# Causal attention of a decoder step on one Trainium2 core: value products over both column halves of the array, denominators added up on VectorE and GpSimd

## The chip, the core and the metric

The kernel runs on one core of one Trainium2 chip: TensorE (matrix products, with its weight loads shown as an engine of their own, PEld), VectorE (DVE), ScalarE (ACT), GpSimd (POOL) and the DMA queues that SyncE (SP) and the others issue. The metric is the device time of one execution in microseconds.

## The reference

One inference step of a one-layer hybrid decoder: 4096 prompt tokens (and 8 sample tokens) pass an RMSNorm and one input projection; the results feed causal attention with a forget gate (6 heads of 64), a state-space group and a cross-attention over 256 memory tokens; an output projection joins them. The change touches only the causal attention over the prompt:

```python
def fox_attend(q, c_q, q_pos, k, v, c_k):
    s = jnp.einsum('bqhd,bkhd->bhqk', q, k).astype(jnp.float32) * (HEAD_DIM ** -0.5)
    s = s + jnp.swapaxes(c_q, 1, 2)[..., :, None] - jnp.swapaxes(c_k, 1, 2)[..., None, :]
    causal = jnp.arange(k.shape[1])[None, :] <= q_pos[:, None]
    s = jnp.where(causal, s, -jnp.inf)
    p = jax.nn.softmax(s, axis=-1)
    return jnp.einsum('bhqk,bkhd->bqhd', p.astype(v.dtype), v)
```

Here c is the running sum of the log forget gates. All is in float32.

## The kernel before

The program is a chain of stages with a barrier between them: `project_prompt`, `forget_gates`, `fox_prompt` (the attention), `memory_prompt`, `ssm`, `sample_attend`, `mix_out`. Only `fox_prompt` changes. It runs from about 1151 us to 2677 us of the span.

For each of 6 heads the queries are cut into 8 blocks of 512 columns (`b`), the keys into 32 tiles of 128 rows (`j`). Block `b` needs tiles 0 to 4b+3, so a head has 144 tiles, 6 heads 864. On the last four tiles of each block only the columns from `q0` = 0, 128, 256, 384 on are computed: of the 864 tiles 720 are 512 wide and 48 each are 384, 256 and 128 wide. Each tile passes three engines:

- TensorE, scores: two products into one of two banks, L1020 (split keys `kst` by the high part `qhi` of the queries) and L1021 (`kone` by the rest `qlo`, whose row 64 carries the negated maximum of each query), and on diagonal tiles a mask (L1023).
- ScalarE, L951: exponential of the bank into one of three buffers `p`.
- TensorE, value product, L1004 in `weighted`: `vone` holds 64 value columns and 64 columns of ones, so that one float32 product of the tile gives outputs on partitions 0 to 63 and the denominators on 64 to 127, summed in a bank of 512 columns. Each float32 product appears in the trace as two MATMUL records.

The maximum of each query must be known before its block starts. `first_pass` (L991) computes the scores once more with the queries on the partitions, in 144 chunks a head, into three banks in turn (`NPRE` = 3); VectorE takes each chunk's maximum (`maxima`, L872) and frees the bank; the four maxima of a block (L876) are turned into a row by TensorE (L979), copied (L879 `mrow`) and brought into `qlo` by a DMA of SyncE (L776). TensorE issues up to three chunks behind each score tile, for the block after the next; in the last block of a head and before its start the chunks of the next head's first blocks.

At a block's end `finish` on VectorE takes the reciprocal of the denominators (L885, 64x512), multiplies (L887), applies the gate (L891), and SyncE stores. `split_q` (L855, L857, L858), `split_k` (L847, L849) and `k_one` (L864) prepare operands, also on VectorE. TensorE's order is score tile n, chunks, value product of tile n-1. Five heads run in a loop, the sixth is written out.

GpSimd meanwhile computes the constant tables of the state-space stage (`ssm_c.tables`, most of it through the helper line L285): many small instructions and some of up to 1024 columns.

## Time and profile before

| What | us |
|---|---|
| median of 3 runs (4040.92 to 4050.84) | 4041.15 |
| the profiled execution, its own time | 4048.91 |
| its span (first to last instruction) | 4047.3 |
| TensorE busy, whole span | 3509.0 (87%) |
| VectorE busy, whole span | 1693.8 (42%) |
| ScalarE busy, whole span | 1008.7 (25%) |
| GpSimd busy, whole span | 652.7 (16%) |

Busy times of one engine overlap for a matmul and the next, so TensorE's share says that it has work in flight, not how full the array is. The granted TensorE clock is 0.901 of full speed over the span. The attention is a bit over a third of the span, and its engines are read there, in stretches, and not from the page's averages.

### The profile page before, as it was taken

The page shows a single profiled execution, that of the slowest core. Times are in us where ns is not written, and L with a number is a line of the kernel's source. Part 1 is how long each engine was busy: PE and PEld are TensorE (multiplying, and loading weights), DVE is VectorE, ACT ScalarE, POOL GpSimd, SP SyncE. Part 2 cuts the span into 40 slices and gives each one's busy share as a digit, 9 for nine tenths or more (in the row PEclk, how much of TensorE's full clock was granted, in tenths as well). Part 3 has the DMA queues.
Part 4 walks back from the last instruction along what each step waited for, and adds up shares of the span by engine and source line. Part 5 has one row for each costly group of instructions (what it writes and reads, how often), then busy time and mean ns, then how long its engine had stood idle before and what let it go on. Part 6 is the DMA issues. An engine that isn't in the chain of part 4 may idle for free. (4 is left out here: it accounts for less than half of the span.)

```text
span 4047.3 us, 44763 instructions
## 1 busy us (share of the span) xinstructions
PE 3509.0 (87%) x14216; PEld 2459.2 (61%) x14216; DVE 1693.8 (42%) x2594; ACT 1008.7 (25%) x1791; POOL 652.7 (16%) x1265
## 2 busy tenths in 40 slices
PE   5999999999949989999899999967767766598999
PEld 4987879879835545555555555534335542376766
DVE  4132131141137567374664747427534542323232
ACT  1112121111113433434344343423201110212120
POOL 0000000000047776500000000000046620000000
PEclk9998999989969999999999999987786777698989
DMA  3241232322141122210101001032156541442322
GB/s 100 94 141 71 86 125 90 124 84 94 68 71 49 50 70 79 61 26 20 39 20 34 22 18 30 3 122 62 42 164 177 157 139 51 121 125 86 124 86 73
DMA packets 236613, 323.67 MB, mean 80 GB/s; under 512 B 100484, under 2 KB 168748, under 8 KB 235380
## 3 DMA queue, kind: packets, MB, share of 16 engines
q1 hardware_dynamic: 175028, 203.79, 17.8%
q10 hardware_dynamic: 49488, 68.48, 4.6%
q0 software_dynamic: 11904, 48.87, 3.6%
q8 instruction: 116, 1.90, 0.2%
q14 instruction: 77, 0.63, 0.0%
HBM read 221.37 MB, written 99.61 MB: 79 GB/s over the span
## 5 line engine op out<-in xcount | busy, mean ns | idle before, releaser
L1004 PE MATMUL bank<-p,vone 128*128 128x512 f32 (+1 forms) x1728 | 862.2, 581 | 10.3 <-ACT p L951 9.7
L951 ACT ACTIVATE p<-bank,ncol 128x512 f32<-128x512 f32 (+1 forms) x864 | 562.1, 651 | 817.0 <-PE bank L1021 647.1
L1020 PE MATMUL bank<-qhi,kst 128*128 128x512 f32 (+1 forms) x864 | 644.0, 745 | 14.1 <-issue 12.6
L872 DVE TENSOR_REDUCE pm<-bank 128x1 f32<-128x512 f32 (+2 forms) x864 | 516.9, 640 | 264.1 <-PE bank L991 195.2
L535 PE MATMUL bank<-xhi,whi 128*128 128x512 f32 x1024 | 408.0, 398 | 7.0 <-DVE xlo L502 7.0
L535 PE MATMUL bank<-xlo,whi 128*128 128x512 f32 x1024 | 406.9, 397 | 0.0
L535 PE MATMUL bank<-xhi,wlo 128*128 128x512 f32 x1024 | 406.9, 397 | 0.0
L1004 PEld LDWEIGHTS bank<-p,vone 128*128 128x128 f32 x1728 | 321.4, 198 | 72.7 <-issue 13.3
L991 PE MATMUL bank<-kone,qone 66*128 66x512 f32 (+2 forms) x864 | 294.6, 413 | 61.6 <-DVE qlo L858 33.9
L476 DVE CAST whi<-wraw 128x3072 fp32r<-128x3072 f32 (+2 forms) x32 | 52.1, 1629 | 703.5 <-PE bank L535 703.5
L1021 PE MATMUL bank<-qlo,kone 66*128 66x512 f32 (+1 forms) x864 | 335.9, 389 | 0.0
L1020 PEld LDWEIGHTS bank<-qhi,kst 128*128 128x128 f32 x864 | 169.2, 196 | 194.4 <-issue 163.2
L1021 PEld LDWEIGHTS bank<-qlo,kone 66*128 66x128 f32 x864 | 169.0, 196 | 177.7 <-issue 170.9
L885 DVE RECIPROCAL rec<-bank 64x512 f32<-64x512 f32 x48 | 161.2, 3359 | 229.4 <-PE bank L1004 228.3
L991 PEld LDWEIGHTS bank<-kone,qone 66*128 66x128 f32 x864 | 166.5, 200 | 111.9 <-issue 53.8
L535 PEld LDWEIGHTS bank<-xhi,whi 128*128 128x128 f32 x1024 | 194.5, 190 | 54.1 <-issue 8.6
L535 PEld LDWEIGHTS bank<-xlo,whi 128*128 128x128 f32 x1024 | 195.1, 191 | 46.1
L535 PEld LDWEIGHTS bank<-xhi,wlo 128*128 128x128 f32 x1024 | 194.5, 190 | 45.7
L2198 PE MATMUL bank<-wo_hi,mx_hi 128*128 128x512 f32 x512 | 205.6, 402 | 0.8 <-DVE wo_raw L2104 0.8
L2198 PE MATMUL bank<-wo_lo,mx_hi 128*128 128x512 f32 x512 | 203.2, 397 | 0.0
L2198 PE MATMUL bank<-wo_hi,mx_lo 128*128 128x512 f32 x512 | 203.1, 397 | 0.0
L569 ACT ACTIVATE fstage<-bank 128x512 f32<-128x512 f32 x104 | 62.2, 598 | 524.3 <-PE bank L535 524.3
(387 smaller groups left out, 4725.5 us busy)
## 6 DMA issues: line engine op xcount, KB each, us to landing
wraw<-in_w_in SPq DMA_DIRECT2D x20, 1536.0 KB, 6.7
ssm_consts<-gp POOLq DMA_DIRECT2D x6, 3080.0 KB, 10.2
x_tok<-in_x_prompt SPq DMA_DIRECT2D x8, 2048.0 KB, 11.2
gate_t<-fstage ACTq DMA_DIRECT2D x32, 512.0 KB, 2.6
mx_x<-in_x_prompt SPq DMA_DIRECT2D x32, 512.0 KB, 3.5
out_y_prompt<-mx_xo ACTq DMA_DIRECT2D x32, 512.0 KB, 2.9
q<-q_t SPq DMA_DIRECT2D x96, 128.0 KB, 3.0
ssm_turns<-ssm_consts SPq DMA_DIRECT2D x24, 512.0 KB, 3.7
```

The source lines that it names most:

```text
L476: dve.tensor_copy(whi[:, si % 2, :, 0:w], wraw[:, :, 0:w]).then_inc(whi_done, 1)
L535: last = pe.matmul(dst, lhsT, rhs, start=(k == 0 and ws is whi and xs is xhi), stop=(k == KD - 1 and ws is wlo))
L569: act.activation(fstage[:, slot, 512 * h:512 * (h + 1)], bank[:], func, scale=1.0 if scale is None else scale).then_inc(evac_done, 1)
L872: dve.tensor_reduce(pm[:, r, ch:ch + 1], c.bank[XB + n % NPRE][:, 0:w], AX.X, ALU.max).then_inc(pre_max, 1)
L885: dve.reciprocal(rec[:], ob[HD:P, :]).then_inc(o_rec, 1)
L951: act.activation(p[:, n % 3, q0:512], c.bank[n % SB][:, q0:512], ACT.Exp, bias=ncol[:, j:j + 1]).then_inc(ex, 1)
L991: mm = pe.matmul(bank[:, 0:w], qone[:, b % QS, q], kone[:, 512 * ch:512 * ch + w], start=True, stop=True)
L1004: pe.matmul(c.bank[OB + b % 2][:, q0:512], vone[:, j, :], p[:, n % 3, q0:512], start=(j == 0), stop=(j == 4 * b + 3), skip_group_check=Tru ...
L1020: pe.matmul(bank[:, q0:512], kst[:, j * P:(j + 1) * P], qhi[:, b % QS, q0:512], start=True, stop=False)
L1021: mm = pe.matmul(bank[:, q0:512], kone[:, j * P:(j + 1) * P], qlo[:, b % QS, q0:512], start=False, stop=True)
L2198: mm = pe.matmul(c.bank[4 + 2 * (t % 2) + h][:], ms_[:, j, k, t * P:(t + 1) * P], ws_[:, k, 512 * h:512 * (h + 1)], start=(k == 0 and ws_ ...
```

## The change

`fox_prompt` is rewritten in steps of four tiles. In words:

- A value product is two products of 64 stationary columns (`v_tok`, without the ones) and at most 256 moving columns: query columns 0 to 255 of the block go to output partitions 0 to 63, columns 256 to 511 to partitions 64 to 127 of the same bank (`weighted`). A tile whose `q0` is 256 or more has only the second. The order on TensorE is: four score tiles with their chunks, then the four value products of the step before.
- The denominators are no longer part of the product. VectorE adds each tile of `p` into `acc_dve` (`add_up`; the first tile of a block is copied); in heads 3 to 5, from block 1 on, the tiles with j % 4 == 1 (105 in all) are added by GpSimd into `acc_pool` and `merge` adds the two. Two products with ones (`denominators`) then sum over the partitions. GpSimd starts on its share behind the tables.
- `finish` works on 128x256 in place of 64x512.
- `p` has 12 buffers in place of 3; the queries have 5 in place of 4.
- A table (`FoxPlan`) places the 144 chunks of a head: they begin 20 tiles ahead, at a rate of 1.14 to a tile, so that tiles 106 to 123 of each head have none. The row of maxima of blocks 5, 6 and 7 is turned in the step before the block's first, in the other blocks earlier.
- All six heads are written out; `split_k` is cut into eight pieces.

The diff, cut to its core:

```diff
+class FoxPlan:
+    STEP = 4
+    def __init__(self, nh, nb, lead, num, den):
+        self.nb = nb
+        self.main = [(b, j, max(0, (j - 4 * b) * P)) for b in range(nb) for j in range(4 * b + 4)]
+        self.pre = [(b, r, ch, 512 if ch < b else (r + 1) * P) for b in range(nb) for r in range(4) for ch in range(b + 1)]
+        self.per = len(self.main)
+        assert len(self.pre) == self.per
+        self.total = nh * self.per
+        self.blocks = nh * nb
+        self.start = [sum(4 * x + 4 for x in range(b)) for b in range(nb + 1)]
+        self.chunks_at, self.rows_at, self.split_at = {}, {}, {}
+        for g in range(self.blocks):
+            h, b = divmod(g, nb)
+            when = [max(-1, self.per * h + (m * den) // num - lead) for m in range(self.start[b], self.start[b + 1])]
+            for m, t in zip(range(self.start[b], self.start[b + 1]), when):
+                self.chunks_at.setdefault(t, []).append(self.per * h + m)
+            self.rows_at.setdefault(when[-1] // self.STEP + 1 if when[-1] >= 0 else -1, []).append(g)
+            self.split_at.setdefault(when[0] // self.STEP - 1 if when[0] >= self.STEP else -1, []).append(g)
+            assert when[-1] // self.STEP + 1 < self.first(g) // self.STEP or g == 0
...
+    QS, PS, GS = 5, 12, 4
+    plan = FoxPlan(NF, NB, 20, 114, 100)
+    NMN, PER, NBLK = plan.total, plan.per, plan.blocks
+    POOL_FROM = 3
+    STEP, NST = plan.STEP, plan.total // plan.STEP
+    def on_pool(n):
+        h, b, j, q0 = plan.tile(n)
+        return h >= POOL_FROM and b > 0 and j % STEP == 1
+    pool_done, dve_done = [0], [0]
+    for n in range(NMN):
+        pool_done.append(pool_done[-1] + on_pool(n))
+        dve_done.append(dve_done[-1] + (not on_pool(n)))
...
-        vone = sb("vone", [P, NT, P])
-        gate = sb("gate_a", [HD, T])
-        ncol = sb("ncol", [P, NT])
-        p = sb("p", [P, 3, 512])
+        vt = sb("v_tok", [P, NT, HD])
+        gate = sb("gate_a", [P, GS, 256])
+        p = sb("p", [P, PS, 512])
+        accd, accp = sb("acc_dve", [P, 2, 512]), sb("acc_pool", [P, 2, 512])
...
-        rec = sb("rec", [HD, 512])
-        on = sb("on", [HD, 512])
-        og = sb("og", [HD, 2, 512])
+        rec = sb("rec", [P, 256])
+        on = sb("on", [P, 256])
+        og = sb("og", [P, 2, 256])
...
+            for n in range(NMN):
+                if not on_pool(n):
+                    continue
+                h, b, j, q0 = plan.tile(n)
+                g = NB * h + b
+                pool.wait_ge(ex, n + 1)
+                k = pool_done[n]
+                if j == 1:
+                    if g >= 2:
+                        pool.wait_ge(merged, g - 1)
+                    pool.tensor_copy(accp[:, g % 2, :], p[:, n % PS, :]).then_inc(accp_done, 1)
+                else:
+                    pool.wait_ge(accp_done, k)
+                    pool.tensor_tensor(accp[:, g % 2, q0:512], accp[:, g % 2, q0:512], p[:, n % PS, q0:512], ALU.add
+                                       ).then_inc(accp_done, 1)
...
+            def add_up(n):
+                h, b, j, q0 = plan.tile(n)
+                g = NB * h + b
+                if not on_pool(n):
+                    dve.wait_ge(ex, n + 1)
+                    k = dve_done[n]
+                    if j == 0:
+                        if g >= 2:
+                            dve.wait_ge(den, g - 1)
+                        dve.tensor_copy(accd[:, g % 2, :], p[:, n % PS, :]).then_inc(accd_done, 1)
+                    else:
+                        dve.wait_ge(accd_done, k)
+                        dve.tensor_tensor(accd[:, g % 2, q0:512], accd[:, g % 2, q0:512], p[:, n % PS, q0:512], ALU.add
+                                          ).then_inc(accd_done, 1)
+            def merge(g):
+                n1 = plan.end(g)
+                dve.wait_ge(accd_done, dve_done[n1])
+                if on_pool(n1 - 3):
+                    dve.wait_ge(accp_done, pool_done[n1])
+                    dve.tensor_tensor(accd[:, g % 2, :], accd[:, g % 2, :], accp[:, g % 2, :], ALU.add).then_inc(merged, 1)
+                else:
+                    dve.sem_inc(merged, 1)
+            def finish(g):
+                ob = c.bank[OB + g % 2]
+                dve.wait_ge(den, g + 1)
+                dve.reciprocal(rec[:], ob[:, 256:512]).then_inc(o_rec, 1)
+                dve.wait_ge(o_rec, g + 1)
+                dve.tensor_tensor(on[:], ob[:, 0:256], rec[:], ALU.mult).then_inc(o_norm, 1)
+                dve.wait_ge(o_norm, g + 1)
+                dve.wait_ge(g_in[g % GS], 32 * (g // GS + 1))
+                if g >= 2:
+                    dve.wait_ge(o_stored[g % 2], 32 * (g // 2))
+                dve.tensor_tensor(og[:, g % 2, :], on[:], gate[:, g % GS, :], ALU.mult).then_inc(o_gated, 1)
...
+            for m in range(NST):
+                h, b, j, q0 = plan.tile(STEP * m)
+                for n in range(STEP * m, STEP * (m + 1)):
+                    for x in plan.chunks_at.get(n, []):
+                        maximum(x)
+                for x in (plan.rows_at.get(m, []) if m else []):
+                    row(x)
+                for x in plan.split_at.get(m, []):
+                    split_q(x)
+                if m:
+                    for n in range(STEP * (m - 1), STEP * m):
+                        add_up(n)
+                    if plan.ended(m - 1):
+                        merge(plan.block(m - 1))
+                if m >= 2 and plan.ended(m - 2):
+                    finish(plan.block(m - 2))
+                if h + 1 < NF and b == NB - 1:
+                    split_k(h + 1, j // KG)
+                    if j >= KG:
+                        k_one(h + 1, j // KG - 1)
+                if h and b == 0:
+                    k_one(h, NG - 1)
...
+            for n in range(NMN):
+                h, b, j, q0 = plan.tile(n)
+                act.wait_ge(sc, n + 1)
+                if n >= PS:
+                    act.wait_ge(pv, n - PS + 1)
+                    act.wait_ge(accd_done, dve_done[n - PS + 1])
+                    if pool_done[n - PS + 1]:
+                        act.wait_ge(accp_done, pool_done[n - PS + 1])
+                act.activation(p[:, n % PS, q0:512], c.bank[n % SB][:, q0:512], ACT.Exp, bias=c.negc[:, h, j:j + 1]).then_inc(ex, 1)
...
+            def weighted(n):
+                h, b, j, q0 = plan.tile(n)
+                g = NB * h + b
+                pe.wait_ge(ex, n + 1)
+                if j == 0 and g >= 2:
+                    pe.wait_ge(o_norm, g - 1)
+                for hf in range(2):
+                    lo, hi = max(q0, 256 * hf), 256 * (hf + 1)
+                    if lo < hi:
+                        mm = pe.matmul(c.bank[OB + g % 2][HD * hf:HD * (hf + 1), lo - 256 * hf:256], vt[:, j, :], p[:, n % PS, lo:hi],
+                                       start=(j == 0), stop=(j == 4 * b + 1 + 2 * hf), skip_group_check=True)
+                mm.then_inc(pv, 1)
+            def denominators(g):
+                pe.wait_ge(merged, g + 1)
+                for hf in range(2):
+                    mm = pe.matmul(c.bank[OB + g % 2][HD * hf:HD * (hf + 1), 256:512], c.ones[:, 0:HD],
+                                   accd[:, g % 2, 256 * hf:256 * (hf + 1)], start=True, stop=True, skip_group_check=True)
+                mm.then_inc(den, 1)
...
+            def values(m):
+                if m and plan.ended(m - 1):
+                    denominators(plan.block(m - 1))
+                for n in range(STEP * m, STEP * (m + 1)):
+                    weighted(n)
...
-            ROWS_AT = (13, 18, 26)
...
+                for x in (plan.rows_at.get(m, []) if m else []):
+                    maxima_to_rows(x)
+                for n in range(STEP * m, STEP * (m + 1)):
+                    h, b, j, q0 = plan.tile(n)
...
+                    for x in plan.chunks_at.get(n, []):
+                        first_pass(x)
+                if b == NB - 1 and h + 1 < NF and j > KG:
+                    turn_k(h + 1, j // KG - 1)
+                if h and b == 0:
+                    turn_k(h, NG - 1)
+                if m:
+                    values(m - 1)
+            values(NST - 1)
+            denominators(NBLK - 1)```

Where the instructions stand. TensorE before, in the last block of the loop's body: a score tile of two products (L1020, L1021) and one value product (L1004) in turn.

```order
L1004 MATMUL bank<-p,vone 128x512
L1020 MATMUL bank<-qhi,kst 128x512
L1021 MATMUL bank<-qlo,kone 128x512
L1001 REGISTER_ALU
L1004 MATMUL bank<-p,vone 128x512
L1020 MATMUL bank<-qhi,kst 128x512
L1021 MATMUL bank<-qlo,kone 128x512
```

And now one step on TensorE, in block 5 of the second head (L1141 and L1142 are the score products, L1087 the chunks, L1103 the value products):

```order
L1141 MATMUL bank<-qhi,kst 128x512
L1142 MATMUL bank<-qlo,kone 128x512
L1087 MATMUL bank<-kone,qone 128x512 x2
L1141 MATMUL bank<-qhi,kst 128x512
L1142 MATMUL bank<-qlo,kone 128x512
L1087 MATMUL bank<-kone,qone 128x512
L1141 MATMUL bank<-qhi,kst 128x512
L1142 MATMUL bank<-qlo,kone 128x512
L1087 MATMUL bank<-kone,qone 128x512
L1141 MATMUL bank<-qhi,kst 128x512
L1142 MATMUL bank<-qlo,kone 128x512
L1087 MATMUL bank<-kone,qone 128x512
L1103 MATMUL bank<-p,v_tok 64x256 x8
```

The value products have gathered at the step's end, eight of 64x256 where four of 128x512 stood between the score tiles.

VectorE, around the end of a block: before, maxima, and the three instructions of `finish` between them.

```order
L871 REGISTER_ALU
L872 TENSOR_REDUCE pm<-bank 128x1
L883 REGISTER_ALU
L885 RECIPROCAL rec<-bank 64x512
L887 TENSOR_TENSOR on<-bank,rec 64x512
L888 REGISTER_ALU
L890 REGISTER_ALU
L891 TENSOR_TENSOR og<-on,gate_a 64x512
L871 REGISTER_ALU
L872 TENSOR_REDUCE pm<-bank 128x1
```

And now (L938 is a maximum, L949 the row's copy, L960 and L963 the adding up, L978 to L985 `finish`):

```order
L938 TENSOR_REDUCE pm<-bank 128x1 x4
L949 CAST mrow<-bank 4x128
L960 COPY acc_dve<-p 128x512
L963 TENSOR_TENSOR acc_dve<-acc_dve,p 128x512 x3
L978 RECIPROCAL rec<-bank 128x256
L980 TENSOR_TENSOR on<-bank,rec 128x256
L985 TENSOR_TENSOR og<-on,gate_a 128x256
L938 TENSOR_REDUCE pm<-bank 128x1 x5
L963 TENSOR_TENSOR acc_dve<-acc_dve,p 128x512 x4
```

Between two groups of maxima VectorE now has four additions to make, and the next chunks of TensorE wait for the maxima behind them.

## Rows read from the trace of the kernel before

**Rows 1.** Table by stretch: before, during and after the attention's tile loop.

```profile
core 0: us, PE busy (x) PEld busy (x) DVE busy (x) ACT busy (x) POOL busy (x), PEclk, DMA share, GB/s
1160.00:1210.00 50.00, 24.70 (x78) 15.35 (x78) 29.37 (x61) 4.78 (x8) 29.40 (x73) 0.50 0.56 89
1210.00:2672.00 1462.00, 1373.85 (x4873) 824.65 (x4873) 858.81 (x1297) 590.55 (x909) 364.71 (x810) 0.96 0.13 36
```

**Rows 2.** Waits in 1210 to 2670 us: total, times, longest (us).

```profile
ACT p L951 <- PE bank L1021: 647.1, 630, 7.8
DVE pm L872 <- PE bank L991: 193.4, 259, 8.5
...
PE bank L991 <- DVE pm L872: 10.5, 18, 1.3
```

**Rows 3.** Timeline of TensorE late in the last head: start us, us, instruction.

```profile
2655.74 1.02 PE L1004 MATMUL bank<-p,vone 128*128 128x512 f32 x2
2656.20 0.79 PE L1020 MATMUL bank<-qhi,kst 128*128 128x512 f32 x1
...
2657.07 1.02 PE L1004 MATMUL bank<-p,vone 128*128 128x512 f32 x2
```

**Rows 4.** The same with two chunks (L991) to a tile.

```profile
2052.24 1.02 PE L1004 MATMUL bank<-p,vone 128*128 128x512 f32 x2
...
2053.58 0.63 PE L991 MATMUL bank<-kone,qone 66*128 66x512 f32 x2
2054.04 0.59 PE L1004 MATMUL bank<-p,vone 128*128 128x512 f32 x1
```

**Rows 5.** Timeline of TensorE in the memory stage: four products on alternate row halves.

```profile
2767.66 1.13 PE L1276 MATMUL bank<-mem_kt,mem_q 64*128 64x256 f32 x8
```

**Rows 6.** Timeline of VectorE, no GpSimd work beside it.

```profile
1999.70 1.29 DVE L872 TENSOR_REDUCE pm<-bank 128x1 f32<-128x512 f32 x2 [0.72 <-PE bank L991]
...
2004.34 0.40 DVE L855 CAST qhi<-q 128x512 fp32r<-128x512 f32 x1
2004.78 0.42 DVE L857 CAST qone<-qhi 64x512 fp32r<-64x512 f32 x1
2005.12 0.68 DVE L858 TENSOR_TENSOR qlo<-q,qhi 64x512 fp32r<-64x512 f32 x1
```

**Rows 7.** Groups by shape on VectorE: out<-in xcount | busy us, mean ns | idle before.

```profile
L872 DVE TENSOR_REDUCE pm<-bank 128x1 f32<-128x512 f32 x720 | 466.8, 685 | 212.9 <-PE bank L991 195.2 <-PE bank L994 17.3
L885 DVE RECIPROCAL rec<-bank 64x512 f32<-64x512 f32 x48 | 161.2, 3359 | 229.4 <-PE bank L1004 228.3
L872 DVE TENSOR_REDUCE pm<-bank 128x1 f32<-128x384 f32 x48 | 26.5, 552 | 15.0 <-PE bank L994 14.8
L872 DVE TENSOR_REDUCE pm<-bank 128x1 f32<-128x256 f32 x48 | 20.3, 422 | 21.7 <-PE bank L994 21.6
L864 DVE CAST kone<-kst 64x512 fp32r<-64x512 f32 x48 | 19.8, 412 | 0.0
L872 DVE TENSOR_REDUCE pm<-bank 128x1 f32<-128x128 f32 x48 | 13.5, 282 | 14.5 <-PE bank L994 14.5
```

**Rows 8.** The subtraction L858 (two SBUF inputs): ns min/median/max, to 1640 us and after 1900 us.

```profile
L858 DVE TENSOR_TENSOR qlo<-q,qhi x18: 675/774/2818, 1166.6 to 1625.8; 64x512 fp32r<-64x512 f32 x18
...
L858 DVE TENSOR_TENSOR qlo<-q,qhi x22: 675/676/679, 1908.5 to 2550.1; 64x512 fp32r<-64x512 f32 x22
```

**Rows 9.** Timeline of GpSimd and VectorE over one such meeting.

```profile
1512.38 2.40 POOL L285 TENSOR_TENSOR gp<-gp,st_big 128x1024 f32<-128x1024 f32 x1
1512.51 2.82 DVE L858 TENSOR_TENSOR qlo<-q,qhi 64x512 fp32r<-64x512 f32 x1
```

**Rows 10.** GpSimd while it makes the tables (us, busy (x), clock), and its 512-wide addition.

```profile
1160.00:1700.00 540.00, 394.11 (x882) 0.91 0.22 63
...
L285 POOL TENSOR_TENSOR gp<-gp,st_big 128x512 f32<-128x512 f32 x12 | 15.7, 1310 | 0.9
```

**Rows 11.** Table by stretch, a piece of the memory stage; columns as in rows 1.

```profile
2800.00:2900.00 100.00, 77.56 (x326) 41.79 (x322) 71.66 (x162) 33.23 (x131) 0.00 (x0) 0.79 0.24 56
```

More of the change, by code:

```diff
@@ L809, in _ @@
+            load_k(0)
+            load_q(0)
+            load_q(1)
             sp.wait_ge(ones_set, 5)
@@ L932, in _ @@
+            for g in range(NG):
+                split_k(0, g)
+            split_q(0)
+            split_q(1)
+            dve.wait_ge(ones_set, 5)
+            for g in range(NG):
                 k_one(0, g)
             ssm_c.copy_c(dve, c)
-            heads(dve, body)
+            for g in plan.split_at[-1][2:]:
+                split_q(g)
+            for m in plan.chunks_at[-1]:
+                maximum(m)
+            for g in plan.rows_at[-1]:
+                row(g)
+            for m in range(NST):
+                h, b, j, q0 = plan.tile(STEP * m)
+                for n in range(STEP * m, STEP * (m + 1)):
[18 more added lines that the diff above has]
+                    k_one(h, NG - 1)
@@ L936, in _ @@
+            for n in range(STEP * (NST - 1), NMN):
+                add_up(n)
+            merge(NBLK - 1)
+            if plan.ended(NST - 2):
+                finish(NBLK - 2)
+            finish(NBLK - 1)
         @block.scalar
@@ L998, in weighted @@
[L998 to L1017 removed]
+                turns[0] += 1
@@ L1045, in body @@
-                    if n:
-                        weighted(h, n - 1)
-                    if j == 4 * b + 3 and rows_due:
-                        maxima_to_rows(h, b + 2, NG * (h + 1))
-                    if b == LASTB and not last and j and j % KG == 0:
-                        rows = sum(x < j for x in ROWS_AT)
-                        if rows > sum(x < j - KG for x in ROWS_AT):
-                            pe.wait_ge(mrow_done, NB * (h + 1) + rows)
-                        turn_k(h + 1, j // KG - 1)
```

397 lines of the change are left out of this document (166 added, 231 removed).

## Prediction, as put on record before the changed kernel ran

> **What bounds the kernel now.** Start with the table by stretch [rows 1]: the tile loop of the attention takes 1462 us, 36% of the span, and TensorE has work in flight for 1374 of them, VectorE for 859, ScalarE for 591. The clock there is 0.96. The other stages are untouched, so the forecast is this stretch's new length; the setup ahead of it is only reordered and I leave it at nothing. The waits [rows 2] say the same from the other side: ScalarE waits 647 us for scores and VectorE 193 for chunks, while TensorE waits 10.5 for the maxima. TensorE ends last everywhere.
>
> Next, what TensorE's time consists of. Where no chunks run, a tile comes every 1.33 us (2655.74 to 2657.07) [rows 3]; with two chunks every 1.80 (2052.24 to 2054.04) [rows 4]. So a 512-column chunk costs 0.235, the two score products, of the same width, 0.47, and the float32 value product the remaining **0.86 us**. In 512-column equivalents there are 720 + 48 x (0.75 + 0.5 + 0.25) = 792 value products: 681 us, half of the stretch. That is what the change goes for.
>
> **TensorE after.** Whether two half-width products run at once is seen in the memory stage: four float32 products of 256 columns on alternate row halves take 1.13 us together [rows 5]. One behind another they would be 4 x 0.43 = 1.72. Each is two records of 0.215; if the second record of one runs beside the first of the next, five slots are 1.08, and that is about what stands there. I take the same for column halves: nearest row, though no row shows column halves. Terms:
> - the value products fall to half: -341;
> - tiles with q0 of 256 and 384 fill one half only, so save nothing: 48 x (0.43 + 0.215) / 2 = +15;
> - each of the 216 steps of four ends with one record alone (0.215) and empties the array twice, going to half width and back. A product's record is 0.40 long where its successor starts after 0.235 [rows 3, 4], so emptying shows some 0.165; with two of them 0.545 a step, +118 (bounds: 0 and 0.545);
> - denominators: 48 pairs of 0.645, +31.
> 1374 - 341 + 15 + 118 + 31 = **1197 us**, 5.5 a step.
>
> **VectorE after.** It had 603 us to spare and now gets the denominators. All prices are for a full queue, where instructions follow at once:
> - maxima, 864: starts lie 0.61 apart (two end after 1.29, one lasts 0.685) [rows 6, 7]; the narrow ones at their mean less the same 0.08: 720 x 0.61 + 48 x (0.47 + 0.34 + 0.20) = 488;
> - additions: the nearest row has two SBUF inputs and 512 columns, 0.676 [rows 8], and an instruction that waits for the one before starts 0.035 after its end [rows 6]: 0.71. Narrower ones less 0.13 per 128 columns, the slope of the maxima [rows 7]. GpSimd takes 105 tiles (84 full, 21 of 384); 48 are copies. 588 x 0.71 + 27 x 0.58 + 48 x 0.45 + 48 x 0.31 = 470;
> - copies as L855 at 0.44: 21; 21 merges at 0.71: 15;
> - finish: a reciprocal of 512 columns is 3.36 [rows 7], so of 256 columns 1.72 with its wait, and two products of 0.45: 48 x 2.62 = 126 (228 before). If the reciprocal did not scale with columns it would be 79 more;
> - unchanged: L855 to L858 at 0.44 + 0.34 + 0.64 [rows 6], 68; L864 20 [rows 7]. Rows of maxima 21 and key pieces of 256 columns 48 x 0.75 = 36, both priced by the narrow rows of [rows 7].
> Sum: **1265 us**, 5.9 a step. So VectorE becomes the engine that ends last, 68 us above TensorE. In the queue, the next chunks' maxima stand behind the additions, and TensorE behind the maxima, with three banks of lead. While VectorE adds (2.8 us), TensorE makes its value products (2.3), then three chunks with their scores (2.1): it arrives first, and VectorE finds three chunks waiting. So the engines do overlap in steady state, and the sum is a good floor there. Twelve buffers of `p` cover ScalarE's lead, and ScalarE (0.69 a tile, 2.8 a step) is never last.
>
> **What the floor lacks.** First, GpSimd. While it works on its tables [rows 10], L858 takes 0.774 in the median in place of 0.676, up to 2.818 [rows 8]. The rows of one meeting show why: beside a table instruction of 2.40 it waits 2.14 of its 2.82 [rows 9], so about the other's length less 0.26. The 882 table instructions are 394 us busy [rows 10]; if each were met by an addition, it would cost 394 - 882 x 0.25 = 174 us (upper bound; lower bound 0). They come every 0.61 us. In a step there are four additions, each letting one of them through, and some 3 us of maxima, which read PSUM and let five pass. Four ninths of 174 is 78: **+80**, spread over the first 98 steps or so, before GpSimd's own share starts with the fourth head (step 108). The 105 additions on GpSimd (about 1.31 each [rows 10]) come while VectorE is at maxima, and I cost them at nothing; without that cover they would cost up to 105 x 1.06 = 111. The Trainium skill has a rule against this change here (SBUF — State Buffer, § SBUF: two separate sides): the port pair that VectorE and GpSimd share is an exclusive lock for an instruction with two SBUF inputs, and the loser blocks for the whole of it. The long meeting agrees; the narrow ones cost 0.10, less than the 0.34 of such an instruction. By the rule in full, with every addition met, the sum would have 174 where I put 80.
>
> Second, places where neither engine's sum holds: the row of maxima of blocks 5 and 6 is made one step before the block, and its DMA (issue 0.7, some 2 to land, by the other small ones: an estimate) keeps TensorE until about the end of the additions, so that VectorE waits 1.3: 12 times, 16. The last 38 tiles have no chunks, TensorE's 4.1 a step against 2.7: 14. The first short blocks of each head with a row, a finish and a split nearly every step, 5 a head: 25 with the remainder; and in heads 3 to 5 VectorE (5.5 a step) and TensorE (5.5) are level, so each one's delays pass to the other: 10. Together **+65**.
>
> Sum: 1265 + 80 + 65 = 1410 against 1462, -52. The profiled execution's own time of 4048.9 becomes 3997; it is 7.8 above the median shown, from which I count: 4041.2 - 52 = **3989 us**.
>
> **Rivals.**
> 1. Tighter than I think (0.18). The emptying costs little, additions mostly meet narrow table instructions (40), and the unequal places cost 30: 1265 + 70 = 1335, 3914. For it: the long table instructions, which carry the excess, are few. Against it: GpSimd always has the next one ready.
> 2. GpSimd decides (0.20): slower. Every table instruction of length meets an addition, 174 in place of 80, for 1504 and **4083**. The gain is gone from the point where the meetings cost over 132, three quarters of the bound. For it: L855, L857 and L858 in a row each waited in turn, as in [rows 9], and additions come in rows of four. Against it: 5 of 9 table instructions have the maxima to run in. The TensorE clock could do the same: where TensorE had pauses, in the memory stage, its clock was 0.79 [rows 11] against 0.96 in the loop [rows 1], and it will have pauses of about 0.4 a step. At 0.8 its 1197 become some 1440 and 4070 is reached.
> 3. The column halves do not run together, so the change doesn't do what it says (0.10). Then TensorE has 1374 + 216 x 0.33 + 48 x 0.86 = 1487, with 65 for waits 1552: +90, **4131**. Against it: the row halves [rows 5].
>
> **How the numbers follow.** The forecast has 0.52, rivals 0.18, 0.20 and 0.10. 0.3% of the time, about what a measurement can tell, is 12 us. The forecast's own range is 3925 to 4045 (table meetings 0 to 130, places 40 to 90), of which 0.07 lies within the 12 us: faster 0.45 + 0.18, about 0.63; same 0.08; slower 0.29. The range for 8 in 10 takes in most of rivals 1 and 2 and leaves the third out: **3900 to 4100**.
>
> **What would show it.** Right: VectorE over 90% busy in the loop and TensorE's longest waits on the maxima (L938); L1103's eight records of a tile pair in about 0.43 us a tile; additions (L963) of 0.68 after step 110 and of 0.8 and more before, some over 2; tables ending later than before, at some 700 us after the loop's start; the loop at about 1410. Wrong: value products that need 0.86 a tile (rival 3); VectorE with gaps of a microsecond before maxima in most steps, or a clock under 0.9 in the loop; a reciprocal over 2 us.

## The result: 0.45% slower, and the profile after

| What | before | after |
|---|---|---|
| median of 8 runs each, us | 4046.27 (4040.92 to 4055.53) | 4065.9 (4048.62 to 4075.19) |
| ratio | | 1.0045, 95% interval 1.003 to 1.006 |
| the profiled execution, its own time | 4048.9 | 4066.9 |
| its span | 4047.3 | 4065.2 |
| tile loop, first score product to last gate product | 1463.4 | 1481.7 |
| granted TensorE clock over the span | 0.901 | 0.873 |

The forecast was 3989 (3900 to 4100), faster. The range holds the result; the sign is wrong. The loop alone explains the difference: it is 18 us longer, the median 20. Everything that follows is about these 1482 us, against the 1410 that I had worked out for them.

The table by stretch of the changed kernel, cut at the starts of heads 0, 1, 2 and 3 (heads are counted from 0); columns as in [rows 1]:

```profile
core 0: us, PE busy (x) PEld busy (x) DVE busy (x) ACT busy (x) POOL busy (x), PEclk, DMA share, GB/s
1205.00:1486.00 281.00, 226.34 (x1092) 137.06 (x1092) 243.33 (x362) 97.03 (x151) 221.66 (x408) 0.82 0.18 57
1486.00:1769.00 283.00, 223.54 (x1114) 134.89 (x1112) 251.55 (x377) 97.71 (x152) 208.67 (x370) 0.84 0.18 57
1769.00:2014.00 245.00, 217.52 (x1117) 132.80 (x1113) 214.26 (x378) 97.55 (x152) 0.00 (x0) 0.87 0.11 27
2014.00:2687.00 673.00, 603.90 (x3288) 370.72 (x3288) 586.15 (x996) 287.81 (x449) 117.72 (x105) 0.93 0.10 24
```

Heads 0 and 1 take 281 and 283 us, head 2 takes 245, heads 3 to 5 together 673. The kernel before needed 251, 252, 244 and 717 for the same. So nothing is won in head 2, 44 us are won in the last three heads, and 61 are lost in the first two, where GpSimd is busy with its tables. VectorE is busy for 1295 us of the 1482 (87%), where it was 859 [rows 1].

The waits in the loop say who holds whom (total us, times, longest), and stand against [rows 2]:

```profile
ACT p L1048 <- PE bank L1142: 585.0, 276, 8.0
...
PE bank L1087 <- DVE pm L938: 147.9, 76, 8.4
...
DVE pm L938 <- PE bank L1087: 62.4, 93, 2.3
...
DVE khl L912 <- DMA ktok<-out_k_prompt: 14.2, 5, 3.7
```

TensorE now waits 148 us for the maxima, where it waited 10.5; VectorE still waits 62 for chunks. VectorE's groups by shape in the loop (xcount | busy us, mean ns | idle before), which answer to [rows 7]:

```profile
L963 DVE TENSOR_TENSOR acc_dve<-acc_dve,p 128x512 f32<-128x512 f32 x588 | 470.1, 799 | 53.7 <-ACT p L1048 8.7 <-DVE acc_dve L963 1.4
L938 DVE TENSOR_REDUCE pm<-bank 128x1 f32<-128x512 f32 x706 | 454.9, 683 | 76.9 <-PE bank L1087 62.4 <-PE bank L1090 6.5 <-DVE nm L943 0.5
L978 DVE RECIPROCAL rec<-bank 128x256 f32<-128x256 f32 x48 | 84.0, 1751 | 6.0 <-PE bank L1110 5.3
```

The additions (L963) are as dear as the maxima. Of the idle time before them, 53.7 us, only 10 has a releaser. The timeline of VectorE in head 4, with no table instruction anywhere, shows what the rest is (start us, us, instruction):

```profile
2302.70 2.47 DVE L938 TENSOR_REDUCE pm<-bank 128x1 f32<-128x512 f32 x4
...
2305.29 2.26 DVE L963 TENSOR_TENSOR acc_dve<-acc_dve,p 128x512 f32<-128x512 f32 x3
2307.47 2.67 DVE L938 TENSOR_REDUCE pm<-bank 128x1 f32<-128x512 f32 x5
```

Four maxima, which overlap, end after 2.47: (2.47 - 0.69) / 3 = 0.59 apart. Three additions need 2.26: (2.26 - 0.69) / 2 = 0.79 apart, longer than each of them lasts. Over the loop the median distance of two 512-wide additions in a row is 0.796 us (390 pairs; with the narrower ones of the diagonal tiles there are 507): each waits for the sum that the one before it writes, and starts 0.10 us after its end. Counted over the loop, with those behind a block's first copy and before a merge, 563 such gaps hold 57 us.

Beside the tables it is a different matter. VectorE and GpSimd in one step of head 0:

```profile
1250.66 9.09 DVE L963 TENSOR_TENSOR acc_dve<-acc_dve,p 128x512 f32<-128x512 f32 x4
1259.68 2.34 DVE L938 TENSOR_REDUCE pm<-bank 128x1 f32<-128x512 f32 x4
```

```profile
1249.88 1.90 POOL L285 TENSOR_TENSOR gp<-gp,uc 128x1024 f32<-128x1024 f32 x1
1251.86 2.23 POOL L285 TENSOR_TENSOR st_big<-gp,us 128x1024 f32<-128x1024 f32 x1
1254.17 2.73 POOL L285 TENSOR_TENSOR gp<-gp,st_big 128x1024 f32<-128x1024 f32 x1
1256.98 2.23 POOL L285 TENSOR_TENSOR gp<-gp,uc 128x1024 f32<-128x1024 f32 x1
```

Four additions take 9.09 us in place of 3.1, since each lets one table instruction of 1024 columns pass. The four maxima right behind, which read PSUM, take their usual 2.34 beside two more such instructions.

GpSimd waits as well. Its most frequent table instruction in the kernel before, and in the changed one:

```profile
L285 POOL TENSOR_TENSOR gp<-gp,st_big 128x64 f32<-128x64 f32 x156 | 53.0, 340 | 12.2
```

```profile
L285 POOL TENSOR_TENSOR gp<-gp,st_big 128x64 f32<-128x64 f32 x156 | 64.9, 416 | 12.2
```

All its table instructions together (885 and 884 from 1100 us on) are busy for 478 us where they were 402. That the additions do this shows in run 6 below, which has none: there the 884 table instructions take 395 us.

TensorE does what was forecast. The four value products of a step in head 4:

```profile
2303.86 1.95 PE L1103 MATMUL bank<-p,v_tok 128*64 128x256 f32 x16
2305.74 0.50 PE L1141 MATMUL bank<-qhi,kst 128*128 128x512 f32 x1
```

16 records in 1.88 until the next product starts: 0.47 us a tile in place of 0.86.

### The profile page after: what moved, and what is told of

Its sections match the earlier page's. It is cut to its first block and busy times, and to the rows that moved or that the text cites. A ratio compares the mean times of both kernels' runs of the same rounds, so it can differ in the third digit from the quotient of the medians.

```text
span 4065.2 us, 46870 instructions
## 1 busy us (share of the span) xinstructions
PE 3408.6 (84%) x15944; PEld 2409.0 (59%) x15944; DVE 2131.4 (52%) x3410; ACT 1001.1 (25%) x1787; POOL 844.5 (21%) x1369
## 3 DMA queue, kind: packets, MB, share of 16 engines
q1 hardware_dynamic: 182708, 203.80, 17.7%
## 5 line engine op out<-in xcount | busy, mean ns | idle before, releaser
L1048 ACT ACTIVATE p<-bank,negc 128x512 f32<-128x512 f32 (+1 forms) x864 | 557.0, 652 | 874.7 <-PE bank L1142 585.0
L938 DVE TENSOR_REDUCE pm<-bank 128x1 f32<-128x512 f32 (+2 forms) x864 | 513.3, 638 | 92.0 <-PE bank L1087 62.4
L963 DVE TENSOR_TENSOR acc_dve<-acc_dve,p 128x512 f32<-128x512 f32 (+3 forms) x711 | 520.0, 731 | 66.9 <-ACT p L1048 9.1
L1087 PE MATMUL bank<-kone,qone 66*128 66x512 f32 (+2 forms) x864 | 365.4, 440 | 174.1 <-DVE pm L938 152.5
L1103 PE MATMUL bank<-p,v_tok 128*64 128x256 f32 (+1 forms) x3264 | 489.9, 434 | 0.0
L1141 PE MATMUL bank<-qhi,kst 128*128 128x512 f32 (+1 forms) x864 | 394.4, 456 | 27.7 <-DMA qlo<-mrow 18.9
L1103 PEld LDWEIGHTS bank<-p,v_tok 128*64 128x64 f32 x3264 | 265.9, 157 | 189.4 <-issue 89.3
L1142 PE MATMUL bank<-qlo,kone 66*128 66x512 f32 (+1 forms) x864 | 341.6, 395 | 0.0
L1087 PEld LDWEIGHTS bank<-kone,qone 66*128 66x128 f32 x864 | 178.7, 209 | 246.1 <-DVE pm L938 183.1
L1141 PEld LDWEIGHTS bank<-qhi,kst 128*128 128x128 f32 x864 | 173.8, 201 | 163.9 <-ACT p L1048 64.8
L900 POOL TENSOR_TENSOR acc_pool<-acc_pool,p 128x512 f32<-128x512 f32 (+1 forms) x84 | 104.8, 1248 | 407.3 <-ACT p L1048 407.3
```

The source lines that it names most:

```text
L900: pool.tensor_tensor(accp[:, g % 2, q0:512], accp[:, g % 2, q0:512], p[:, n % PS, q0:512], ALU.add).then_inc(accp_done, 1)
L938: dve.tensor_reduce(pm[:, r, ch:ch + 1], c.bank[XB + m % NPRE][:, 0:w], AX.X, ALU.max).then_inc(pre_max, 1)
L963: dve.tensor_tensor(accd[:, g % 2, q0:512], accd[:, g % 2, q0:512], p[:, n % PS, q0:512], ALU.add).then_inc(accd_done, 1)
L1048: act.activation(p[:, n % PS, q0:512], c.bank[n % SB][:, q0:512], ACT.Exp, bias=c.negc[:, h, j:j + 1]).then_inc(ex, 1)
L1087: mm = pe.matmul(bank[:, 0:w], qone[:, g % QS, r * P:(r + 1) * P], kone[:, 512 * ch:512 * ch + w], start=True, stop=True)
L1103: mm = pe.matmul(c.bank[OB + g % 2][HD * hf:HD * (hf + 1), lo - 256 * hf:256], vt[:, j, :], p[:, n % PS, lo:hi], start=(j == 0), stop=(j = ...
```

## The experiments

The theory after this look: **VectorE sets the loop, and three things lengthen its queue**: additions that wait for one another, additions that wait for table instructions, and times in which it has no finished chunk. The rivals: the new order costs TensorE more than I counted, or its clock does; or it is the placing of the chunks.

In the table, "against the change" is the ratio less 1.0045, times 4046 us. Two intervals go into each, so that it is good to about 12 us. "Loop" is from the profiled execution, counted as above. The runs came in three groups of four; the kernel before ran beside each group (medians of 4043.7, 4047.6 and 4047.9 us), and the ratios are to that.

| Kernel | median us | ratio to before (95%) | against the change | loop |
|---|---|---|---|---|
| 1 five of six table rounds left out | 3996.9 | 0.9875 (0.9849 to 0.9901) | -69 | 1425 |
| 2 two accumulators in turn | 3968.5 | 0.9808 (0.9782 to 0.9833) | -96 | 1385 |
| 3 additions between the maxima | 3999.1 | 0.9878 (0.9851 to 0.9906) | -68 | 1421 |
| 4 both halves on the same columns | 4172.0 | 1.0315 (1.0288 to 1.0342) | +109 | 1588 |
| 5 kernel before, tables as in 1 | 4041.2 | 0.9981 (0.9969 to 0.9993) | | 1447 |
| 6 no additions | 3824.0 | 0.9445 (0.9425 to 0.9464) | -243 | 1230 |
| 7 as 2, GpSimd from head 2 on | 3967.8 | 0.9788 (0.9764 to 0.9812) | -104 | 1384 |
| 8 as 7, GpSimd two tiles of four | 3970.8 | 0.9798 (0.9776 to 0.9820) | -100 | 1394 |
| 9 chunks at 1.30 a tile | 4052.1 | 1.0010 (0.9993 to 1.0027) | -14 | 1468 |
| 10 as 1 and 2 together | 3902.6 | 0.9645 (0.9611 to 0.9678) | -162 | 1319 |
| 11 as 2 and 3 together | 3973.4 | 0.9809 (0.9783 to 0.9835) | -96 | 1392 |
| 12 as 2, GpSimd adds nothing | 3987.0 | 0.9848 (0.9821 to 0.9874) | -80 | 1408 |

### 1 and 5: the table instructions, and their control

```diff
-        for g0 in range(0, G, m_):
+        for g0 in (0,):
```

The one result is stored for all groups.

> The changed kernel with one of the six rounds of GpSimd's table work left: the other five rounds are left out, so the state-space outputs are not the reference's. Theory GpSimd (the meetings of additions with table instructions made heads 0 and 1 of the changed kernel 281 and 283 us long against 245 for head 2, which has no GpSimd work): heads 0 and 1 fall to about 245 to 250, total -65 to -75, near 3995. Rival (the row of maxima, the clock or the burst order cost the time in heads 0 and 1): less than -20.

> The kernel before, with five of the six rounds of GpSimd's table loop left out (their results are replaced by the first round's, so the state-space part of the output is not the reference's). It is the control of the run with few tables. Theory A (the 69 us that the changed kernel won without the tables come from additions of VectorE that meet table instructions): the kernel before has hardly any two-input instructions on VectorE in the loop and TensorE ends last, so it gains under 5 us: 4039 to 4046 beside a before of about 4044, with a loop of 1460 to 1465. Theory B (the tables cost something that has nothing to do with the additions, as HBM traffic or a lower TensorE clock): it gains a good part of the 69 too, 3980 to 4020.

-69 us for the changed kernel, as expected, and -8 for the kernel before (4046 x 0.0019), a little over the 5 that theory A allowed and nothing like the 24 to 64 of theory B. So about 60 us of the 69 belong to the changed kernel alone. The loops of the profiled executions give less: 57 us and, for the kernel before, 16 (1447, where 1460 to 1465 were expected), which leaves 41. Each loop is that of a single execution, and 13 executions of the kernel before spread over 21 us. That it is VectorE's instructions meeting table instructions, additions above all, is seen in their lengths: what all its instructions of heads 0 and 1 last over the median of their shape in head 2 falls from 76 us to 10. Head 0 falls from 281 to 257 us, head 1, which has no table instruction left, from 283 to 242. Its VectorE shows additions at their own length (head 1 of run 1, one line of the groups), where the same line of heads 0 and 1 of the changed kernel has a mean of 950:

```profile
L964 DVE TENSOR_TENSOR acc_dve<-acc_dve,p 128x512 f32<-128x512 f32 x112 | 77.1, 689 | 8.8
```

```profile
L963 DVE TENSOR_TENSOR acc_dve<-acc_dve,p 128x512 f32<-128x512 f32 x219 | 207.9, 950 | 17.7 <-DVE acc_dve L963 0.5
```

### 2: two accumulators in turn

```diff
-        accd, accp = sb("acc_dve", [P, 2, 512]), ...
+        accd, accp = sb("acc_dve", [P, 4, 512]), ...
...
-                        dve.wait_ge(accd_done, k)
-                        dve.tensor_tensor(accd[:, g % 2, q0:512], ...
+                        dve.wait_ge(accd_done, k - 1 if b else k)
+                        dve.tensor_tensor(accd[:, d, q0:512], ...
```

`d` alternates between two buffers of the block, so that the first two tiles of a block are copied and not the first alone (90 copies and 546 additions of 512 columns in place of 48 and 588); `denominators` issues its products for both and sums them in the bank.

> VectorE adds alternate tiles into two accumulators, and TensorE sums both, so that no addition reads what the one before wrote. Theory dependency (an addition behind an addition starts 0.794 us after it, where I had priced 0.71, since it waits for the semaphore of its predecessor): starts fall to about 0.61 to 0.65, as the maxima's, and the total by 60 to 90 us less some 30 of added products on TensorE that is partly idle: 3980 to 4020. Rival (VectorE and TensorE take turns in bursts of four, and VectorE's saving only becomes more waiting for chunks): -25 or less.

Of the single changes that keep the additions it gains most, -96 us, and more than the expected 3980 to 4020 allowed. The timeline of VectorE in this run:

```profile
2290.12 1.29 DVE L938 TENSOR_REDUCE pm<-bank 128x1 f32<-128x512 f32 x2
2291.32 1.89 DVE L965 TENSOR_TENSOR acc_dve<-acc_dve,p 128x512 f32<-128x512 f32 x3
2293.12 3.07 DVE L938 TENSOR_REDUCE pm<-bank 128x1 f32<-128x512 f32 x5
```

Three additions end after 1.89 in place of 2.26: 0.602 apart in the median, as close as maxima. 0.796 - 0.602 = 0.194 for each of the 563 pairs would be 109; 96 came out, and of these some 11 belong to the 42 tiles that are copied now (in this run the next instruction starts 0.34 us after a copy and 0.60 after an addition). An estimate for the dependence alone is thus 85 us. The gaps between additions fall from 57 to 3 us.

### 3 and 11: each addition behind one tile's maxima

```diff
                     for x in plan.chunks_at.get(n, []):
                         maximum(x)
+                    if m:
+                        add_up(n - STEP)
...
-                    for n in range(STEP * (m - 1), STEP * m):
-                        add_up(n)
```

> VectorE's order alone is changed: behind each tile's maxima one addition of the step before, in place of all maxima of a step and then four additions. It takes away the dependent pairs and the bursts at once. Theory bursts: -60 to -100 us and TensorE's waits for maxima (148 us in the loop) fall under 60. If only the dependency counts: about the same as the two accumulators, -50. Rival GpSimd: more additions meet table instructions since they are spread over the whole step, heads 0 and 1 stay at 280.

> Two accumulators in turn and, besides, each addition behind one tile's maxima in place of four in a row. Theory A (with independent additions nothing is left for the interleaving to take away, and the finer order only lets VectorE run out of finished chunks more often, 151 us of large idle times against 109 in the run that interleaved alone): no gain or a loss, 3965 to 3985 beside the 3968.5 of the run with two accumulators. Theory B (additions between maxima meet fewer table instructions in a row and free the banks earlier, so TensorE stops less in the first two heads): 3935 to 3955.

Run 3 takes the waits between additions away by other means (gaps of 57 us fall to 9), and gains 68, not 96. TensorE's waits for the maxima fall from 148 us to 91, not under 60, and heads 0 and 1 take 250 and 262 us, so they did not stay at 280. VectorE's waits of over 0.15 us grow from 109 to 151 us, which I put down to its asking for chunks earlier in each step; no run separates this. Run 11 adds nothing to two accumulators, as theory A said: both changes cure the same cost.

### 4: do the column halves run together?

```diff
-                        mm = pe.matmul(c.bank[OB + g % 2][HD * hf:HD * (hf + 1), ...
+                        mm = pe.matmul(c.bank[OB + g % 2][HD * (hf if j == 0 else 0):HD * ((hf if j == 0 else 0) + 1), ...
```

From the second tile of each block on, both halves go to partitions 0 to 63, so the value sums are not the reference's; the count and width of all products is the same.

> From the second tile of each block on, both halves of a value product go to partitions 0 to 63, so both use the same column half of the array; the outputs are wrong. If column halves do run together in the changed kernel: a step's 16 records take about 3.5 us in place of 1.95, TensorE ends last, and the total rises by 150 to 250 us. If they did not run together, nothing changes.

+109 us, less than the expected 150 to 250. The four value products of a step (TensorE, head 4) now need 3.18 in place of 1.95 (expected: 3.5):

```profile
2320.27 3.18 PE L1103 MATMUL bank<-p,v_tok 128*64 128x256 f32 x16
```

0.80 us a tile against 0.49: the halves do run together in the changed kernel. In head 3 of this run TensorE ends last again, at a granted clock of 0.98:

```profile
2070.00:2320.00 250.00, 242.38 (x1120) 152.79 (x1122) 202.05 (x351) 97.90 (x153) 38.39 (x35) 0.98 0.12 26
```

### 6: TensorE's own floor

```diff
+    def adds(n):
+        return plan.tile(n)[2] == 0
```

`add_up` is called for these tiles alone, the first of each block; the other 816 additions are left out, on both engines, and with them the 21 merges. The first tile's copy is written as an addition of a constant.

> The changed kernel without its additions: of each block only the first tile goes into the accumulator, the other 816 tiles are left out of the denominators, on VectorE and on GpSimd, so the outputs are not the reference's. What is left is TensorE's own floor. Theory A (the new TensorE order is cheap, VectorE's additions hold it back): VectorE's sum falls by some 440 us below TensorE's, and the loop is about what I had put for TensorE with small waits, 1197 + 40 to 60 = 1240 to 1260 in place of 1482, the whole 3820 to 3850. Theory B (TensorE in the new order has stalls of its own, by emptying twice a step or by the row DMA): the loop stays above 1330, the whole above 3915.

3824 us, with a loop of 1230. The loop by stretch (head 0, head 1, heads 2 to 5):

```profile
1205.00:1428.00 223.00, 205.24 (x1092) 128.20 (x1092) 147.46 (x234) 96.93 (x151) 170.73 (x380) 0.89 0.20 60
1428.00:1634.00 206.00, 192.90 (x1116) 121.30 (x1114) 139.58 (x242) 97.53 (x152) 150.11 (x371) 0.98 0.24 75
1634.00:2435.00 801.00, 758.35 (x4399) 478.20 (x4398) 510.81 (x903) 385.19 (x601) 29.90 (x35) 0.97 0.13 32
```

TensorE needs some 200 us a head where it hardly waits for VectorE (22 us for maxima over the loop). My sum for it was 1197, the loop is 33 more, a little less than the 40 to 60 that I expected for its waits. The additions, their merges included, are the whole loss: 252 us of the changed kernel's loop go with them.

### 9: are the chunks placed too unevenly?

```diff
-    plan = FoxPlan(NF, NB, 20, 114, 100)
+    plan = FoxPlan(NF, NB, 20, 130, 100)
```

> The changed kernel with its chunks spread at a rate of 1.30 to a tile in place of 1.14 (the same work, only placed more unevenly: some 33 of 144 tiles a head have no chunks, where it is 18). Theory A (the term that I mis-sized is this unevenness: where chunks run VectorE ends last, where none run TensorE does, and three banks can't level it out; half of VectorE's large idle times, 50 of 109 us, lie in the last block of each head): about four more steps a head in which TensorE needs some 1.2 us more than VectorE, five times 4 x 1.2 = 24 us, VectorE's large idle times grow from 109 to 125 to 150, the whole 4080 to 4100 beside the 4065.9 of the changed kernel. Theory B (VectorE's work alone sets the end, or the row DMA does): 4055 to 4075.

**A miss.** It is 14 us faster than the change, where theory A wanted it 14 to 34 slower; VectorE's waits of over 0.15 us stay where they were (109.5 us against 109.0), and its row in the waits is no longer than before:

```profile
DVE pm L938 <- PE bank L1087: 49.9, 59, 3.1
```

With 33 tiles a head without chunks in place of 18 VectorE is idle no longer than before, so these tiles are not what leaves it idle. The run is also 3 us below the range of theory B, and why it is faster than the change stays open.

### 10: both cures at once

> Both of the costs that I have named taken away at once: two accumulators in turn, and five of the six rounds of GpSimd's table loop left out (the state-space part of the output is not the reference's). Theory A (they are separate costs on VectorE): the gains of 97 and 69 us add up less what TensorE takes over as the new floor (its heads of 201 to 207 without additions): heads 0 and 1 fall from 258 and 260 to some 220 to 230, the loop from 1385 to 1310 to 1330, the whole 3895 to 3915. Theory B (they are one and the same slack, or TensorE and its clock are already the limit): over 3940.

-162 us, and -69 - 96 = -165 by the single runs: two separate costs. The loop is 1319 (head 0: 239, where 220 to 230 were expected, heads 1 and 2: 222 each, heads 3 to 5: 218, 214 and 204). What is left over TensorE's floor of 1230 is 89 us.

### 7, 8 and 12: GpSimd's share

```diff
-    POOL_FROM = 3
+    POOL_FROM = 2
...
-        return h >= POOL_FROM and b > 0 and j % STEP == 1
+        return h >= POOL_FROM and b > 0 and j % STEP in (1, 3)
```

Run 7 has the first edit, run 8 both, run 12 has `POOL_FROM = 6`; all on top of run 2.

> The run with two accumulators in turn, with GpSimd taking its quarter of the tiles from the third head on in place of the fourth. GpSimd was idle in the third head (0 us busy there in the trace of the changed kernel), and VectorE had all the additions to make. Theory A (VectorE ends last in the third head): 35 additions of 0.60 to 0.70 go from VectorE, less a merge of 0.7 for each of 7 blocks: 16 to 20 us of the third head's 234, the whole 3950 to 3955 beside the 3968.5 of the run with two accumulators. Theory B (with two accumulators TensorE already ends last from the third head on): under 6 us.

> As the run before, with GpSimd taking two tiles of every four (j % 4 of 1 and 3) from the third head on. Theory A (VectorE ends last and GpSimd can carry more): another 35 additions of 0.60 a head leave VectorE, some 20 us each in four heads, until TensorE's own 205 or so a head is the floor: heads of 205 in place of 216, 214 and 204, so 15 to 35 us below the run with a quarter, 3920 to 3940. Theory B (GpSimd's additions of 1.31 lie beside VectorE's and each meeting makes VectorE wait, or the merge waits for GpSimd): as many meetings as in the first two heads, VectorE's additions above 0.80 in the mean, and no gain or a loss: 3950 to 4000.

> Two accumulators in turn, and no tile for GpSimd at all: VectorE makes all additions. Theory A (GpSimd's additions cost VectorE nothing, and VectorE ends last in the heads 3 to 5, as I forecast): it gets 105 additions of 0.60 to 0.69 back less 21 merges of 0.7, some 50 to 55 us, and the heads 3 to 5 go from 216, 214 and 204 to some 230, the whole 4005 to 4025. Theory B (taking a second quarter over to GpSimd, and a first one in the third head, both changed nothing, so VectorE isn't what those heads wait for, or what GpSimd takes is given back in waiting for the shared memory port): 3965 to 3985.

Run 7 is 8 us below run 2, with intervals that overlap: it can't be told from nothing, where I expected 16 to 20. Run 8 gains nothing more, where theory A wanted 20 to 35. Run 12 is 16 above run 2 and 24 above run 7, at 3987 nearly where theory B had its upper end (3985) and not at the 4005 to 4025 of theory A; its interval overlaps that of run 2 and stands clear of that of run 7. So GpSimd's share is worth some 20 us, where its additions would be 50 on VectorE. The reason why the second quarter is worth nothing shows in VectorE's additions of heads 3 to 5 (ns min/median/max), a quarter on GpSimd (run 7), then half (run 8):

```profile
L965 DVE TENSOR_TENSOR acc_dve<-acc_dve,p x276: 273/678/1773, 1978.0 to 2579.0; 128x512 f32<-128x512 f32 x116, 128x256 f32<-128x256 f32 x11, 128x128 f32<-128x128 f32 x11
```

```profile
L965 DVE TENSOR_TENSOR acc_dve<-acc_dve,p x175: 292/679/1774, 1974.2 to 2586.9; 128x512 f32<-128x512 f32 x146, 128x256 f32<-128x256 f32 x23, 128x384 f32<-128x384 f32 x3, 128x128 f32<-128x128 f32 x3
```

276 fall to 175, but the 512-wide ones that are left have a mean of 0.88 to 0.90 us in these heads in place of 0.69 to 0.72 (49 or 50 of them a head against 77 to 79), and VectorE is busy for 190 us in head 4 where it was 191. GpSimd's additions of 1.3 us, two to a step, are met as the tables are: counted as in run 1, the meetings take 18 to 20 us of each of these heads in run 8, 2 to 4 in run 7, and none in run 12.

## Why the prediction was wrong

**Right.** VectorE became the engine that ends last, and TensorE waits for the maxima. The column halves run together (run 4), so the third rival fell. TensorE's 1197 was 1230 without additions (run 6). The maxima are 0.59 to 0.61 apart, the reciprocal takes 1.75 (priced at 1.72), and the meetings with table instructions cost 41 to 76 us: 69 - 8 by the medians of runs 1 and 5, 57 - 16 by their loops, 76 by adding up what all VectorE instructions of heads 0 and 1 last over the median of their shape in head 2, 57 of it in the additions. The term was 80. Rival 2, which had them at 174, fell with it, though its 4083 is the figure nearest to the measured time. Of the signs, some failed: VectorE is 87% busy and not over 90, the tables end 537 us after the loop's start and not 700, and the clock in the loop is 0.88, which I had named as a sign of being wrong (under 0.9).

I priced the narrow meetings at nearly nothing and the long ones in full, and the rows bear that out: of 220 512-wide additions in heads 0 and 1 (108 and 112), 160 last 0.7 us, 12 last 0.8, 4 last 1.0 to 1.2, and 44 last 1.35 to 2.7. The Trainium skill (SBUF — State Buffer, § SBUF: two separate sides) calls the shared port pair an exclusive lock, by which the loser, the one that comes second, waits for the whole instruction. The 9.09 us of four additions beside four instructions of 1024 columns agree with it. That most additions in these heads last no longer than elsewhere does not speak against it, since GpSimd loses as well: its table instructions took 76 us more than before.

**Wrong** were above all two terms of VectorE's sum, which made the loop 1410 where it is 1482. The account of the changed kernel's VectorE: busy 1295 us, of which 95 are meetings; 57 in gaps between additions; 18 in other gaps under 0.15; 109 in some 133 gaps above that. 1200 + 57 + 18 = 1275 stands against my floor of 1265, 95 against 80, 109 against 65: together 69 of the 72. Of the 95, 76 are met by tables and 19, counted the same way, by GpSimd's own additions in heads 3 to 5, which I had priced at nothing; 8 of these fall on the gate product (L985), whose 25 instructions there have a mean of 0.75 us where head 2 has 0.42.

1. **The step that failed: "an instruction that waits for the one before starts 0.035 after its end [rows 6]: 0.71".** A 512-wide addition with an addition behind it holds VectorE for 0.796. Per pair, the narrower ones too, I was 0.08 to 0.09 short, 507 times, 43 us. (Other terms were too high by some 33, 16 of it on the 156 full additions that have no addition behind them and hold VectorE for 0.61, so that the whole floor was short by only 10.) I had taken the 0.035 from a cast [rows 6] whose successor read what it wrote, and the 0.676 from a subtraction [rows 8] that is the last of its row. Neither row shows two such additions in a row, each on the sum of the other. The error was more than the 43 us: I took 0.71 for the price of an addition, when an addition without the wait costs 0.602 (run 2). The accumulator's dependence was a cost of the change by itself, some 85 of the 96 us that run 2 gains, and I had not listed it as one.

2. **The places where neither engine's sum holds: 65 forecast, 109 measured** in large gaps. The places that I named are there, but one I had not counted: `split_k` of the next head stands in VectorE's queue at the start of block 7 and waits for its keys' DMA, 14 us in 5 waits, up to 3.7 (the row of L912 above). Half of the 109 us lie in block 7 of the heads. I then blamed the tiles without chunks, and run 9 showed that to be wrong. How the rest divides between the row DMA, the short blocks and the coupling of the two engines stays open; the same sort of gaps are in every run here in which VectorE ends last (108 to 153 us, 129 in run 10), so making VectorE's instructions shorter did not remove them.

The granted clock was 0.82 to 0.93 in the changed loop where I had used the one of before, 0.96, in TensorE's 1197. I had named this beside rival 2. It went down where TensorE waited for VectorE (0.82 in head 0), and up to 0.96 for the loop where it did not (run 6). It doesn't set the loop by TensorE's sum: the 1230 of run 6, had at 0.96, would be some 1340 at the loop's mean of 0.88, still 140 below 1482 (an estimate, with all of TensorE's time scaled). The low clock came with the additions and went with them. Whether it lengthens the 109 us of large gaps was not tried.

As to the sign: of the 243 us that the additions cost (run 6), some 162 are the dependence and the tables (run 10), and without either of the two the change is a gain of 1% or more (run 1 is 0.989 of run 5, the kernel before with the same few tables; run 2 is 0.981). Had I priced the 507 pairs at what they cost, the sum would have been 1453 against 1462, which is no difference; the large gaps and the meetings with GpSimd's own additions make it the loss. The range of 3900 to 4100 holds the result by its width alone. The forecast's own range in it, 3925 to 4045, isn't what its bounds give: table meetings of 0 to 130 and places of 40 to 90 add up to 3884 to 4064.

**The version to keep** is run 2: 3968.5 us, 0.9808 (0.9782 to 0.9833) of the kernel before; it computes the whole of the attention. Run 7 is the same within the error.

## What to carry to other kernels

When an accumulation moves from PSUM to VectorE, ask first whether each addition waits for the last: price the chain by a row of two dependent instructions of that very kind, and split it over two accumulators that the product behind them sums, where the engine of that product does not end last. Price a two-input instruction on VectorE by what GpSimd runs beside it, row by row: beside 1024-column instructions it can cost their length, beside narrow ones next to nothing, and the same holds for work moved over to GpSimd to relieve VectorE. And take the added work away altogether in one run: that shows the other engine's floor and how much of the time is at stake.

## What the runs showed of the hardware that was not expected

- On VectorE a float32 addition of 128x512 from SBUF lasts 0.69 us. Two in a row start 0.602 apart where the second does not use the first's result, and 0.796 apart where it does, so the dependence costs 0.19 us, though a wait is written in both kernels.
- Two float32 products of 256 columns on the two column halves of the array run together: 0.47 to 0.49 us for the pair, 0.80 where both go to the same half.
- Two additions on GpSimd of 1.3 us in a step of 4 tiles raise the mean of VectorE's 512-wide additions from 0.69 to 0.89 us; one in a step leaves it at 0.69 to 0.72, and none at 0.68 (run 12).
- Where VectorE's additions and GpSimd's table instructions run side by side, both lose: 76 us on VectorE's instructions in heads 0 and 1, and 76 us on GpSimd's table instructions (478 us in place of 402; 395 in run 6, which has no additions).
